# Router logits from turned x with folded norm weights; normed rows from two spread rows; two weight low halves on GpSimd

## The chip, the cores and the metric

The kernel runs on one core of a Trainium2 chip. The metric is the device time of one execution in microseconds, the median of the runs. The engines are TensorE (PE; its weight loads are PEld), VectorE (DVE), ScalarE (ACT), GpSimd (POOL) and SyncE (SP), which only issues DMAs; ScalarE and GpSimd issue DMAs as well.

## The reference, cut to what matters

Two token groups (256 latent tokens, 128 context tokens; 3 tiles of 128 rows) go through two layers of width 1024. A layer is a mixer (four token mixers, gated merge, output projection) and a mixture of experts, each behind a modulated norm:

```python
mod = silu(cond) @ w_mod + b_mod
sh1, sc1, g1, sh2, sc2, g2 = split(mod, 6)      # per group: c for latent, c_ctx for context
h = rmsnorm(x, norm_mix) * (1 + sc1) + sh1
x = x + g1 * mixer(h)
h = rmsnorm(x, norm_ffn) * (1 + sc2) + sh2
glog = h @ router_group                          # 4 groups, the best one is taken
elog = h @ router_expert                         # 16 experts, the best two of that group
...
gate = softmax weight of the group * normed softmax weights of the two experts
hid = silu(h @ w_gate) * (h @ w_up)
x = x + g2 * sum over experts (hid * gate) @ w_down
```

The change is in how the second `h` and the 20 logits `glog`, `elog` are made.

## The kernel before, in words

**Staging.** Weights come from HBM as units of 128x1024 fp32 (512 KB) through a ring of buffers. Large products are done in split form (`three`): an operand is written as a rounded high half and a low half (operand minus high half), and each product is `hi*hi + hi*lo + lo*hi` in three fp32r matmuls. ScalarE makes a unit's high half, GpSimd (mixer stage, line 812) or VectorE (expert stage, `unit_low`, line 1889) its low half; three units are in work at a time (`CONV`). In the mixer stage a unit takes TensorE about 4 us, in the expert stage about 1.4. The units of the output projection are the last eight of the mixer stage (`("gemm", 94)` to `("gemm", 101)`). After a unit stand the steps that `schedule()` puts there; each engine walks through the same `SCHEDULE` in order and skips what is not its own, so an engine that waits in a step does nothing of the later ones.

**Norm before the experts** (`("norm", 1)`, lines 1000 to 1042, 1444 to 1463, 1935 to 1982). When the projection of a tile is added to x (VectorE, line 1997 and below, `residual(t)`), ScalarE sums its squares, GpSimd makes 1/rms (`rstd`), VectorE and ScalarE scale the rows of x to `xn`. TensorE turns each of 8 chunks of 128 columns (`columns`), VectorE applies scale and shift per column, which now lie on partitions (line 1959), ScalarE and VectorE or GpSimd make high and low halves, TensorE turns the chunk back to rows (`back`), ScalarE copies it to `hn` (line 1021), and TensorE adds the chunk's part of the 20 logits in split form (`router`). Ahead of it TensorE has two groups of modulation products (`quad`, for the first chunks of the next layer; also run in the last layer), and runs of matmuls on the identity (`keep_busy`) fill gaps.

**Routing** (`("route",)`, lines 546 to 646, 1231 to 1238, 1493 to 1523). The logits (20 rows x 384 tokens) are copied by ScalarE, turned by TensorE to token rows and copied by VectorE (line 550). VectorE picks the group; TensorE counts tokens per group by a triangular matmul (line 1520); VectorE makes the selection matrices `sel` (line 579). TensorE then sorts the first 128 rows of group 0 by 24 matmuls `hn` x `sel` (line 1780). Meanwhile VectorE ranks the experts (lines 583 to 593), makes the gates and then the slot of every token in DRAM (to line 622); GpSimd writes `hn` and the gates to these slots with three indirect DMAs (line 888) and loads the next tile's rows `hs` (line 904).

**Experts.** Six tiles of 128 sorted rows, 24 units each: for expert e four gate/up units and two down units. `rows_high` (ScalarE) and `rows_low` (VectorE, line 1893) make the halves of the sorted rows. Order on VectorE at the start: `rows_low(0)`, gates, `rows_low(1)`, slots, low halves of units 3, 4, 5, then the loop with low halves and the hidden products of an expert (lines 2240 and 2244). Unit 8 of a tile is the first down unit (`S<-whi,ehi` in TensorE's rows). TensorE turns the next tile's rows behind unit 18 (line 1744).

**Queues.** SP issues in program order (lines 723 to 750): expert units 0 to 2, the next layer's modulation weights (`next_layer`), units 3 to 5 when the turned `xn` is read, units 6 to 11, then the gate of the experts spread on all partitions (`load_gate`). ScalarE issues the gate scratch stores (`gout`) and the spread of the first gate.

Of the kernel before, what the change touches and what calls it, by code (L numbers as in the profile page):

```python
# [22 lines left out]
F32 = mybir.dt.float32  # L23
# [5 lines left out]
P = 128  # L29
# [38 lines left out]
GRP = 4  # L68
# [29 lines left out]
BUSY_NORM, BUSY_LOGITS, BUSY_RANK, BUSY_PLACE = 5, 3, 5, 6  # L98
# [11 lines left out]
def schedule():  # L110
# [76 lines left out]
    put(36 + 30, ("gt", 0))  # L187
    put(36 + 33, ("gout", 0))
    put(36 + 50, ("gt", 1))
    put(36 + 53, ("gout", 1))  # L190
# [93 lines left out]
def program(nc, a, out, counts):  # L284
# [4 lines left out]
    with ctx:  # L289
# [13 lines left out]
        wlo = sb("wlo", [P, CONV, 1024], F32R)  # L303
        hhi = sb("hhi", [P, KD, TILES * P], F32R)
# [23 lines left out]
        h_sorted = nc.dram_tensor("h_sorted", (NT * P, ROW), F32, kind="Internal").ap()  # L328
        y_sorted = nc.dram_tensor("y_sorted", (NT * P, D), F32, kind="Internal").ap()
# [8 lines left out]
        smhi = sb("smhi", [P, KD, SMALL], F32R)  # L338
        smlo = sb("smlo", [P, KD, SMALL], F32R)
# [36 lines left out]
        rwf = rw[:, :, :].rearrange("p t n -> p (t n)")  # L376
        cond_t = prob[:, 0].rearrange("p a n -> p (a n)")[:, 0:32 * KD].rearrange("p (k c) -> p k c", k=KD)
# [68 lines left out]
        xn_act, hl_pool = sg("xn_act"), sg("hl_pool")  # L446
# [24 lines left out]
        nb_pe, nb_act = sg("nb_pe"), sg("nb_act")  # L471
# [10 lines left out]
        last_sel, last_selT, last_act, last_pe = sg("last_sel"), sg("last_selT"), sg("last_act"), sg("last_pe")  # L482
# [42 lines left out]

        def load_gate(queue, i):

            for c in range(2):
                src = a["g_scratch"][i].rearrange("(j c) n -> c j n", c=2)[c]
                g_in.of(queue.dma_start(gbc[:, c, :].rearrange("p (j n) -> p j n", j=KD),  # L530
                                        bass.AP(src.tensor, src.offset, [[0, P], [2 * P, KD], [1, P]])))
# [14 lines left out]
        def route(dve, need, own, tt, rows_low, next_mods, unit_low):  # L546

            V = nc.vector
            need(rt_pe, 0)
            own(V.tensor_copy(rt[:, :, :], O[:, 0:60].rearrange("p (t n) -> p t n", t=TILES)))  # L550
# [17 lines left out]
            rg_dve.of(tt(rw[:, :, 8:12], gl, b4(gmax), ALU.subtract))  # L568

# [11 lines left out]
            sel_dve.of(ins)  # L581

# [21 lines left out]
            rows_low(1)  # L604

# [20 lines left out]
            for n in range(CONV + 1, LEAD):  # L626
                unit_low(n)
# [22 lines left out]
        def _(sp):  # L650
# [11 lines left out]
            for l in range(layers):  # L662
# [33 lines left out]
                for s in SCHEDULE:  # L696
# [11 lines left out]
                    elif s == ("experts",):  # L708
# [15 lines left out]
                        for j in range(3):  # L724
                            next_layer(j)
# [1725 lines left out]
```

## Time and profile before

| | us |
|---|---|
| median of 3 runs | 1705.46 |
| lowest, highest | 1700.32, 1705.67 |
| the profiled execution | 1706.39 |
| its span, first to last instruction | 1704.8 |

Busy in the span: TensorE 1658.0 us (97%), VectorE 1014.5 (60%), ScalarE 871.0 (51%), GpSimd 657.1 (39%). The granted clock of TensorE was 0.993 of full on average.

A timeline row reads: start in us from the span's start, duration, engine, line of the kernel, operation, output tile <- input tiles, shape, count; in brackets the engine's idle time before it and what ended it. Rows of several instructions are merged; an fp32 matmul of TensorE that isn't a transpose leaves two records. A matmul's duration overlaps the next one's, so the pace is read from the starts. VectorE's rows of helper functions all carry the helper's line (1858), so they are told apart by their tiles. `pA` holds x and the expert units 0 to 2, `pB` the scaled rows and units 3 to 5.

### The profile page before, as it was taken

To read this page: it belongs to the slowest core of one execution; us is meant where nothing else is said; L and a number is where in the kernel's file an instruction comes from. 1 tells how busy PE (TensorE), PEld (TensorE's weight loads), DVE (VectorE), ACT (ScalarE), POOL (GpSimd) and SP (SyncE) were. 2 spreads that over 40 slices of the span, in tenths; PEclk is the share of its full clock that TensorE was granted. 3 is DMA by queue.
4 is the path that set the end of the run, shared out by engine and by line. 5 is a ranking of instruction groups with operands and counts; after the bars stand their busy time and mean duration, and the time that the engine had idled before them with its cause. 6 is when DMAs were issued, how large, how long until landed. Compare 5 with 4: busy or idle time off the path is not lost.

```text
span 1704.8 us, 27109 instructions
## 1 busy us (share of the span) xinstructions
PE 1658.0 (97%) x10021; PEld 1333.3 (78%) x10021; DVE 1014.5 (60%) x1736; ACT 871.0 (51%) x1471; POOL 657.1 (39%) x414
## 2 busy tenths in 40 slices
PE   6999999999999999999989999999999999999997
PEld 5788887777888877777768888777778887777775
DVE  2226567564451189999860384775635314899997
ACT  2443345544533357778634334454544234587884
POOL 0545464334476621001125554534346675111002
PEclk8999999999999999999999999999999999999999
DMA  8833344343556459999865334344354653999994
GB/s 310 284 103 107 107 148 124 106 180 136 206 202 210 173 210 403 373 369 369 310 224 187 99 115 142 107 131 141 131 192 149 244 198 115 365 385 366 372 364 156
DMA packets 120811, 367.13 MB, mean 215 GB/s; under 512 B 11964, under 2 KB 34044, under 8 KB 120704
## 3 DMA queue, kind: packets, MB, share of 16 engines
q1 hardware_dynamic: 95024, 323.99, 52.5%
q0 software_dynamic: 6624, 24.18, 3.8%
q10 hardware_dynamic: 19056, 17.52, 3.3%
q8 instruction: 69, 1.13, 0.3%
q14 instruction: 38, 0.31, 0.1%
HBM read 341.71 MB, written 23.93 MB: 214 GB/s over the span
## 4 chain that ended last, share of the span: by engine, by line
PE 71%; DVE 14%; issue 5%; ACT 4%; DMA 3%; POOL 1%; SPq 1%; ACTq 0%; DVEq 0%; POOLq 0%
PE G L1335 18%; PE G L1337 17%; PE G L1336 17%; DVE wlo L1858 6%; ACT whi L973 3%; DVE pA L1858 2%; PE T L1649 2%; PE O L1392 2%; DMA x_scratch<-pA 2%; PE S L1635 1%; PE O L1680 1%; PE S L1335 1%; DVE prob L1858 1%; PE S L1337 1%; PE S L1336 1%
## 5 line engine op out<-in xcount | busy, mean ns | idle before, releaser
L812 POOL TENSOR_TENSOR wlo<-raw,whi 128x1024 fp32r<-128x1024 f32 x198 | 488.8, 2474 | 561.2 <-ACT whi L965 561.2
L1335 PE MATMUL G<-whi,hhi 128*128 128x512 f32 (+1 forms) x1440 | 579.1, 402 | 11.2 <-DVE wlo L1858 5.4
L1337 PE MATMUL G<-whi,hlo 128*128 128x512 f32 (+1 forms) x1440 | 558.7, 388 | 0.0
L1336 PE MATMUL G<-wlo,hhi 128*128 128x512 f32 (+1 forms) x1440 | 558.4, 388 | 0.0
L1335 PEld LDWEIGHTS G<-whi,hhi 128*128 128x128 f32 x1440 | 271.4, 188 | 89.0 <-DVE wlo L1858 20.8
L1337 PEld LDWEIGHTS G<-whi,hlo 128*128 128x128 f32 x1440 | 271.3, 188 | 57.6
L1336 PEld LDWEIGHTS G<-wlo,hhi 128*128 128x128 f32 x1440 | 271.9, 189 | 47.3
L965 ACT ACTIVATE whi<-raw 128x1024 fp32r<-128x1024 f32 x204 | 214.7, 1054 | 103.2 <-PE G L1337 73.3
L1858 DVE TENSOR_TENSOR wlo<-raw,whi 128x1024 fp32r<-128x1024 f32 x150 | 179.7, 1219 | 6.7 <-ACT whi L973 3.7
L973 ACT ACTIVATE whi<-raw 128x1024 fp32r<-128x1024 f32 x144 | 152.7, 1061 | 33.1 <-PE G L1337 18.5
L973 ACT ACTIVATE whi<-pA 128x1024 fp32r<-128x1024 f32 x72 | 76.4, 1061 | 41.5 <-PE G L1337 22.9
L1858 DVE TENSOR_TENSOR wlo<-pA,whi 128x1024 fp32r<-128x1024 f32 x72 | 87.9, 1223 | 15.7 <-ACT whi L973 13.2
L1175 ACT ACTIVATE prob<-prob,am 128x384 f32<-128x384 f32 x64 | 38.9, 609 | 99.5 <-DVE am L1858 52.8
L1858 DVE TENSOR_TENSOR wlo<-pB,whi 128x1024 fp32r<-128x1024 f32 x72 | 85.3, 1223 | 6.9 <-ACT whi L973 6.3
L1335 PE MATMUL S<-whi,ehi 128*128 128x512 f32 x192 | 79.4, 413 | 6.8 <-DVE elo L1858 6.4
L973 ACT ACTIVATE whi<-pB 128x1024 fp32r<-128x1024 f32 x72 | 75.1, 1057 | 11.1 <-PE G L1337 10.7
L1335 PE MATMUL G<-whi,bhi 128*128 128x512 f32 x192 | 78.3, 408 | 0.0
L1337 PE MATMUL S<-whi,elo 128*128 128x512 f32 x192 | 75.3, 392 | 0.0
L1337 PE MATMUL G<-whi,blo 128*128 128x512 f32 x192 | 75.1, 391 | 0.0
L1336 PE MATMUL S<-wlo,ehi 128*128 128x512 f32 x192 | 75.1, 391 | 0.0
L1336 PE MATMUL G<-wlo,bhi 128*128 128x512 f32 x192 | 74.9, 390 | 0.0
L807 POOL TENSOR_TENSOR sink_col<-ones 128x1 f32<-128x1 f32 x26 | 15.4, 592 | 149.4 <-ACT yo L1271 76.7
(385 smaller groups left out, 2349.9 us busy)
## 6 DMA issues: line engine op xcount, KB each, us to landing
raw<-in_units SPq DMA_DIRECT2D x426, 512.0 KB, 5.0
pA<-in_units SPq DMA_DIRECT2D x78, 512.0 KB, 6.0
pB<-in_units SPq DMA_DIRECT2D x72, 512.0 KB, 6.3
h_sorted<-sig POOLq DMA_DIRECT2D x12, 514.0 KB, 7.2
hs<-h_sorted POOLq DMA_DIRECT2D x10, 514.0 KB, 7.5
y_sorted<-yo POOLq DMA_DIRECT2D x10, 512.0 KB, 7.2
bias<-in_nat_bias ACTq DMA_DIRECT2D x16, 256.0 KB, 3.6
kT<-in_units SPq DMA_DIRECT2D x6, 512.0 KB, 4.7
```

What stands on the lines that cost most here:

```text
L812: lo_done.of(nc.gpsimd.tensor_tensor(wlo[:, k, :], raw[:, POS_OF[g] % RAW, :], whi[:, k, :].bitcast(F32), ALU.subtract))
L965: hi_done.of(nc.scalar.activation(whi[:, g % CONV, :], raw[:, p % RAW, :], ACT.Copy))
L973: hi_done.of(nc.scalar.activation(whi[:, n % CONV, :], expert_raw(n), ACT.Copy))
L1175: e = nc.scalar.activation(prob[:, u % 2, m, lo:lo + w], src, ACT.Exp, bias=am[:, u % 2, i:i + 1], accum_out=am[:, u % 2, 4 + i:5 + i])
L1335: nc.tensor.matmul(dst, st_hi, mv_hi, start=start, stop=False)
L1336: nc.tensor.matmul(dst, st_hi, mv_lo, start=False, stop=False)
L1337: return nc.tensor.matmul(dst, st_lo, mv_hi, start=False, stop=stop)
L1392: mm = nc.tensor.matmul(O[32 * q:32 * q + 32, c0:c0 + P], cond[:, k, :], raw[:, MODPOS[j - MQ + 1 + q] % RAW, k * P:(k + 1) * P], start=(k ...
L1635: nc.tensor.matmul(S[:, m, 0:256], q, kT[r, kj, 0:256], start=True, stop=True)
L1649: mm = nc.tensor.transpose(T[:, m, b * P:(b + 1) * P], prob[:, u % 2, m, b * P:(b + 1) * P], ident[:, :])
L1680: mm = nc.tensor.matmul(O[64 * m:64 * m + 64, to], values(b, lo, 64), pr, **fl)
L1858: return V.tensor_tensor(o, i0, i1, op)
```

## The change

- **Router.** The logits are computed from x itself. Since `h = x * rstd * a + b` (`a = 32 * (1 + sc2) * norm_ffn` per column, `b = sh2`), the logit is `rstd * (x @ (a*W)) + b @ W`. `rsm` = `a*W` is made once per layer for each token group (two VectorE products behind `("modt", 4)`), `b @ W` by 8 small matmuls (`("rbias", 0)`) and spread over the partitions by two more (`("rbias", 1)`). TensorE turns x: the first 512 columns in the new step `("xt",)` between units 100 and 101, the others in `("norm", 1)` as each tile's residual is done. ScalarE copies turned x to `xT`. 24 plain fp32 matmuls with turned x as the stationary side (128x128) and 20 moving columns give the logits with tokens on partitions. The split router, the copy and the turning of the logits go.
- **Rows.** `hn = (x * a_row) * rstd + b_row` on VectorE: `part_row` for half a tile (a product of 128x512), `whole_row` for a tile (one scalar_tensor_tensor of 128x1024). a and b are turned (`("gt", 1)`, `("gt", 2)`), stored to scratch and spread over the partitions by four DMAs on ScalarE's queue (`rowsA`, `rowsB`) into `pB`. Whole row 0 comes behind the part rows, whole row 1 behind the group choice, whole row 2 behind `sel`. Scaling by columns, turning back and the copies to `hn` go in `("norm", 1)`.
- **Low halves.** GpSimd makes those of expert units 1 and 2 (VectorE did before), after whole row 2. VectorE makes unit 0's ahead of the evacuation of the last projection units, unit 3's ahead of the slot arithmetic and unit 4's in the middle of it.
- **TensorE.** The modulation quads run behind the logits and behind the group counts, and in the first layer only. Three of the four runs of `keep_busy` in this stretch go. The gate selection moves behind unit 3 of the first expert tile, which is written out instead of being the loop's first pass.
- **SP.** Units 6 to 11 are asked for before the gate (in the first layer 8 to 10 last, when the quads are read), the gate's spread before units 3 to 5, and these wait for whole row 2. In the last layer the next layer's modulation weights aren't loaded.

```diff
+    for i, at in enumerate((66, 71, 79, 86)):
+        put(at, ("gt", i))
+        put(at + 3, ("gout", i))
+    put(84, ("dma", "rowsA"))
+    put(88, ("rbias", 0))
+    put(90, ("rbias", 1))
+    put(FIRST_UNIT[CHUNK_NO["wout", 0]] + 2, ("dma", "rowsB"))
+    put(FIRST_UNIT[CHUNK_NO["wout", 1]] + 2, ("xt",))
...
# route(), VectorE
-            own(V.tensor_copy(rt[:, :, :], O[:, 0:60].rearrange("p (t n) -> p t n", t=TILES)))
+            own(*(V.scalar_tensor_tensor(rt[:, t, :], logit_bank(t), st[:, t:t + 1], rt[:, t, :],
+                                         ALU.mult, ALU.add) for t in range(TILES)))
...
             rg_dve.of(tt(rw[:, :, 8:12], gl, b4(gmax), ALU.subtract))
+            whole_row(1)
...
             sel_dve.of(ins)
+            whole_row(2)
...
             rows_low(1)
+            low_of_two()
+            unit_low(CONV)
...
             own(V.scalar_tensor_tensor(diff, base, float((GRP - 1) * P), at, ALU.add, ALU.subtract))
+            unit_low(CONV + 1)
...
             need(sg_pe, 0)
-            unit_low(CONV)
             q_gate.of(V.tensor_copy(gate[:, :], O[:, 0:GRP]))
-            for n in range(CONV + 1, LEAD):
+            for n in range(CONV + 2, LEAD):
                 unit_low(n)
...
# SP
+                        for r in (0, 1, 5) if more_layers else range(RAW):
+                            released(last_of(r))
+                            expert_load(RAW + r, RAW)
+                        need(*evacuated(CHUNK_NO["wout", 1], TILES - 1))
+                        sp.wait_ge(*g_out.at(l, 3))
+                        load_gate(sp, 3)
+                        need(router_dve, WHOLE + TILES - 1)
                         for n in range(TILES, RAW):
                             expert_load(n, 0)
+                        if more_layers:
+                            need(nx_pe, NEXT - 1)
+                            for r in (2, 3, 4):
+                                expert_load(RAW + r, RAW)
...
# GpSimd, ("norm", 1)
+                            pool.wait_ge(*router_dve.at(l, WHOLE + TILES - 1))
+                            pool.wait_ge(*e_lo.in_tile(l, 0, UT, 0))
+                            for n in (1, 2):
+                                pool.wait_ge(*hi_done.at(l, NG + n))
+                                e_lo.of(nc.gpsimd.tensor_tensor(wlo[:, n % CONV, :], expert_raw(n),
+                                                                whi[:, n % CONV, :].bitcast(F32), ALU.subtract))
...
# ScalarE, ("xt",) and ("norm", 1)
+                def turned_x(t, hf):
+                    act.wait_ge(*router_pe.at(l, TURNED_X + TILES * hf + t))
+                    router_act.of(nc.scalar.activation(xT[:, 4 * hf:4 * hf + 4, t * P:(t + 1) * P],
+                                                   psum(turn_bank(t, hf)).rearrange("p (c n) -> p c n", c=4), ACT.Copy))
...
# TensorE
+                def turn_x(t, hf):
+                    need(*((ev_pool, pooled(CHUNK_NO["wout", 0], t)) if hf == 0 else residual(t)))
+                    b = turn_bank(t, hf)
+                    free(b)
+                    for c in range(4):
+                        mm = nc.tensor.transpose(psum(b)[:, c * P:(c + 1) * P],
+                                                 x[:, t, (4 * hf + c) * P:(4 * hf + c + 1) * P], ident[:, :])
+                    router_pe.of(mm)
+                    read[b] = (router_act, COPIED_X + TILES * hf + t)
...
+                def logits(t, hf):
+                    need(router_dve, ROUTER_W)
+                    need(router_act, COPIED_X + TILES * hf + t)
+                    for k in range(4 * hf, 4 * hf + 4):
+                        mm = nc.tensor.matmul(logit_bank(t), xT[:, k, t * P:(t + 1) * P], rsm[:, k, t // 2, :],
+                                              start=(k == 0), stop=(k == KD - 1))
+                    return mm
...
# TensorE, ("norm", 1)
+                            for t in range(2):
+                                turn_x(t, 1)
+                            free("O")
+                            for hf in range(2):
+                                for t in range(2):
+                                    logits(t, hf)
+                            turn_x(2, 1)
+                            for hf in range(2):
+                                mm = logits(2, hf)
+                            rt_pe.of(mm)
...
# VectorE
+                def part_row(t, hf):
+                    h = slice(hf * 512, (hf + 1) * 512)
+                    own(tt(hn[:, t, h], x[:, t, h], rows[0][:, t // 2, h], ALU.mult))
...
+                def whole_row(t):
+                    dve.wait_ge(*rstd_pool.at(l, TILES + t))
+                    router_dve.of(V.scalar_tensor_tensor(hn[:, t, 0:D], hn[:, t, 0:D], st[:, t:t + 1], rows[1][:, t // 2, :],
+                                                       ALU.mult, ALU.add))
...
                         if i == n - 1 and kind == "wout":
+                            if arg == 1:
+                                unit_low(0, 0)
                             dve.wait_ge(*g_in.at(l, 1))
```

## Rows read from the trace of the kernel before

**Rows 1.** the page's part 4, shares of the chain that ended last, by engine

```profile
PE 71%; DVE 14%; issue 5%; ACT 4%; DMA 3%; POOL 1%; SPq 1%; ACTq 0%; DVEq 0%; POOLq 0%
```

**Rows 2.** timeline of TensorE, second layer, from the last projection unit on

```profile
1435.43 0.39 PE L1337 MATMUL G<-whi,hlo 128*128 128x512 f32 x1
...
1458.05 2.92 PE L1780 MATMUL T<-prob,hn 128*128 128x128 f32 x24 [0.43 <-DVE prob L579]
...
1464.38 0.49 PE L1335 MATMUL G<-whi,hhi 128*128 128x512 f32 x1
...
1478.09 0.49 PE L1335 MATMUL S<-whi,ehi 128*128 128x512 f32 x1 [1.68 <-DVE elo L1858]
...
1494.29 0.60 PE L1744 MATMUL T<-ident,hs 128*128 128x128 f32 x4
```

**Rows 3.** timeline of TensorE, first layer, the same two edges

```profile
599.22 0.39 PE L1337 MATMUL G<-whi,hlo 128*128 128x512 f32 x1
...
628.17 0.48 PE L1335 MATMUL G<-whi,hhi 128*128 128x512 f32 x1
```

**Rows 4.** timeline of VectorE, second layer, evacuation to expert units 4 and 5

```profile
1433.19 0.69 DVE L1858 TENSOR_TENSOR sig<-G,pC 128x512 f32<-128x512 f32 x1 [12.97 <-PE G L1337]
...
1436.58 0.69 DVE L1858 TENSOR_TENSOR pA<-pA,sig 128x512 f32<-128x512 f32 x1
...
1454.07 0.22 DVE L550 COPY rt<-O 128x60 f32<-128x60 f32 x1
...
1455.35 0.17 DVE L1858 TENSOR_TENSOR rw<-rt,rw 128x12 f32<-128x12 f32 x1
1456.22 0.17 DVE L574 COPY rw<-O 128x12 f32<-128x12 f32 x1 [0.71 <-PE O L1520]
...
1457.82 0.17 DVE L1858 TENSOR_TENSOR rw<-rt,rw 128x16 f32<-128x16 f32 x1
...
1461.63 0.69 DVE L1858 TENSOR_TENSOR hlo<-T,hhi 128x512 fp32r<-128x512 f32 x1
...
1467.57 0.17 DVE L622 TENSOR_SCALAR slot_at<-rw 128x3 int32<-128x3 f32 x1
...
1468.87 2.35 DVE L1858 TENSOR_TENSOR wlo<-pB,whi 128x1024 fp32r<-128x1024 f32 x2
```

**Rows 5.** timeline of TensorE, second layer, transposes between two projection units

```profile
1395.73 0.82 PE L1706 MATMUL T<-ident,pA 128*128 128x128 f32 x6
...
1396.97 0.48 PE L1335 MATMUL G<-whi,bhi 128*128 128x512 f32 x1
```

**Rows 6.** timeline of ScalarE, second layer, high halves of weight units

```profile
1423.67 1.06 ACT L965 ACTIVATE whi<-raw 128x1024 fp32r<-128x1024 f32 x1 [3.02 <-PE G L1337]
...
1466.06 1.06 ACT L973 ACTIVATE whi<-pB 128x1024 fp32r<-128x1024 f32 x1 [1.78 <-PE G L1337]
```

**Rows 7.** the page's part 6, DMA issues: KB each, us to landing

```profile
pB<-in_units SPq DMA_DIRECT2D x72, 512.0 KB, 6.3
...
hs<-h_sorted POOLq DMA_DIRECT2D x10, 514.0 KB, 7.5
```

**Rows 8.** timeline of GpSimd: a low half in the mixer, the row load

```profile
1037.68 2.40 POOL L812 TENSOR_TENSOR wlo<-raw,whi 128x1024 fp32r<-128x1024 f32 x1 [1.28 <-ACT whi L965]
...
1483.46 0.61 POOL L904 DMA_DIRECT2D hs<-h_sorted  x1
```

**Rows 9.** timeline of VectorE beside the low half of the group above

```profile
1038.05 0.15 DVE L1858 TENSOR_TENSOR ms<-S,ms 128x4 f32<-128x4 f32 x1
...
1038.84 1.25 DVE L1858 TENSOR_TENSOR ms<-ms 128x4 f32<-128x4 f32 x1
```

**Rows 10.** busy time by stretch; last columns: PEclk, DMA share, GB/s

```profile
862.00:864.00 2.00, 0.00 (x0) 0.01 (x1) 1.11 (x4) 1.88 (x2) 0.71 (x2) 1.00 0.92 352
864.00:866.00 2.00, 1.95 (x12) 1.57 (x12) 1.42 (x5) 0.45 (x1) 0.00 (x0) 0.73 0.98 365
866.00:870.00 4.00, 2.06 (x5) 1.68 (x6) 4.00 (x9) 1.19 (x4) 0.00 (x0) 0.50 0.95 352
```

More of the change, by code:

```diff
@@ L1454, in _ @@
-                        for c in range(KD if w else 4):
-                            columns(w, c)
-                            if w and c:
-                                back(c - 1)
-                            if w and c > 1:
-                                router(c - 2)
-                        if w:
-                            back(KD - 1)
-                            router(KD - 2)
-                            router(KD - 1)
+                        if w:
+                            for t in range(2):
[8 more added lines that the diff above has]
+                            rt_pe.of(mm)
+                            continue
@@ new lines, in _ @@
+                        keep_busy(S[:, 0, 0:P], BUSY_BEGIN)
+                        need(xn_dve, 1)
+                        need(xn_act, 0)
+                        for c in range(4):
+                            columns(c)
+                    elif s == ("xt",):
+                        for t in range(TILES):
+                            turn_x(t, 0)
+                    elif s == ("rbias", 0):
+                        need(mod_dve, 3)
+                        free("O")
+                        for k in range(KD):
+                            mm = nc.tensor.matmul(O[0:2, 0:NLOG], modc[:, 3, k, :], small[:, k, 16:SMALL],
+                                                  start=(k == 0), stop=(k == KD - 1))
+                        router_pe.of(mm)
+                        read["O"] = (router_act, BIAS_COPY)
+                    elif s == ("rbias", 1):
+                        free("O")
+                        for c in range(2):
+                            mm = nc.tensor.matmul(O[:, c * NLOG:(c + 1) * NLOG], ident[0:2, c:c + 1].to_broadcast([2, P]), qrow,
+                                                  start=True, stop=True)
+                        router_pe.of(mm)
+                        read["O"] = (router_dve, ROUTER_BIAS)
@@ L1746, in turn, with one_tile @@
                                 q_t.of(mm)
-                        def one_tile(i, last):
+                        def one_tile(i, last, first=False):
                             pe.wait_ge(*q_lo.in_tile(l, i, 2, 0))
@@ L1762, in one_tile @@
                                     down(i, e, u - 4)
+                                if n == SELECT_GATES and first:
+                                    need(gates_dve, 0)
+                                    for t in range(TILES):
+                                        mm = nc.tensor.matmul(O[:, 0:GRP], sel[:, t, :], hn[:, t, D:ROW],
+                                                              start=(t == 0), stop=(t == TILES - 1))
+                                    sg_pe.of(mm)
                                 if n in TURN_HID:
@@ L1783, in _ @@
                             q_t.of(mm)
-                        need(gates_dve, 0)
-                        for t in range(TILES):
-                            mm = nc.tensor.matmul(O[:, 0:GRP], sel[:, t, :], hn[:, t, D:ROW],
-                                                  start=(t == 0), stop=(t == TILES - 1))
-                        sg_pe.of(mm)
-                        with pe.Fori(0, NT - 1) as i:
+                        if l < DEPTH - 1:
+                            turned()
+                        one_tile(0, False, True)
+                        with pe.Fori(1, NT - 1) as i:
                             one_tile(i, False)
```

296 lines of the change are left out of this document (143 added, 153 removed).

## Prediction

> **What bounds the kernel now.** I read the chain that ended last first [rows 1]: TensorE carries 71% of it, VectorE 14%, so a stretch is worth what it keeps TensorE from starting. The diff touches one such stretch per layer, between the output projection and the expert matmuls. TensorE's timeline of the second layer [rows 2]: the last projection matmul starts at 1435.43; such matmuls stand 0.23 us apart, so I set E = 1435.66 and count from it. Sorting starts at E+22.4, the first expert matmul at E+28.7, the first down matmul (unit 8) at E+42.4, after 1.68 us of waiting for VectorE. In the first layer the distance is the same, 628.17 - 599.45 = 28.7 [rows 3]. All that the change can touch is some 42 us in each of two layers. I follow it to unit 8, because VectorE paces the first expert tile. VectorE's rows [rows 4] show the order there: evacuation of the projection, 1433.19 to 1437.27; logits taken over at 1454.07; group choice out at 1455.52; counts back at 1456.22; ranking from 1457.82; first low half of the sorted rows at 1461.63; slots at 1467.57.
>
> **Part 1, work moved ahead of E.** TensorE gets 12 transposes (first half of x) between two projection units. The same insertion, 12 transposes between units, took from 1395.73 to 1396.97 [rows 5], and 0.08 for the slower restart: 1.3 us. The logits' shift needs 8 fp32 matmuls with a stationary side of two columns, 16 records; no row shows such. Bounds: nothing, if they slip into the gaps, and 0.117 a record, the pace of the 54 records (24 sorting matmuls, 3 of the gate selection, two records each) between 1458.05 and 1464.38 [rows 2], 1.9 in all. I take 1.0: the nearest row has 128 columns to load and these have two, but each record must still be issued. Two spreading matmuls (4 records, 0.5) and two more transposes of 16 rows (0.1 each by [rows 5]): **3.0 us** per layer, bounds 2.0 to 3.9. This is on the path: TensorE runs those units back to back. Two more scratch stores, four spread loads and the copies lie on ScalarE, which waits about 3 us in every unit [rows 6]: nothing; without that cover some 3 us. VectorE's three products of the first half go where it idles for 12.97 us [rows 4]. They keep the shared port for 3 x 0.69 = 2.1 us from GpSimd, whose low halves are about as much ahead: nothing, at most 0.5 without the cover. SP now loads expert units 3 to 5 when the third whole row is done (E+14.2), behind two spread loads; such a load lands 6.3 us later [rows 7] and ScalarE wants it after unit 0, at about E+25: nothing, with 4 us of cover.
>
> **Part 2, E to sorting.** ScalarE now has three copies of turned x before the high half of expert unit 0, and VectorE makes unit 0's low half ahead of the evacuation, so that starts at about E-0.95 instead of 1433.19 = E-2.5. At (1437.27-1433.19)/3 = 1.36 us a tile the residuals are done at E+0.4, +1.8 and +3.1. TensorE turns tiles 0 and 1 (to E+2.3), then has 16 logit matmuls. A sorting matmul is the nearest, 2 records of 0.117: 0.23 us each, 3.7, to E+6.0; four transposes 0.45; 8 matmuls 1.85: E+8.3, seen by VectorE at E+8.45. Meanwhile VectorE has three half products (0.72 each with their waits) and whole row 0, E+3.1 to E+6.6: hidden. A whole row costs what a low half of the same 1024 elements does, 2.35/2 = 1.2 us [rows 4]. From the logits to the group choice it was 1.45 us, now 1.65 (three instructions for one copy): E+10.1. Whole row 1 takes 1.2 and covers the wait of 0.70 for the counts: E+11.3. From there to sorting it was 1458.05 - 1456.22 = 1.83; whole row 2 adds 1.2: sorting starts at **E+14.35, 8.05 us earlier**. The old norm on turned rows (16 scalings, 8 highs, 8 lows, 24 transposes back, 24 split matmuls) is gone from the path; the second layer's two modulation quads, gone too, lay beside other work.
>
> **Part 3, sorting to the first expert matmul.** Before: 1458.05 to 1464.38, 6.3 us. The gate selection (6 records, 0.7) moves behind unit 3, so TensorE could start 5.6 after 14.35, at E+20.0. But GpSimd's two low halves are released by whole row 2, just when the ranking starts, and one takes 2.4 us [rows 8]. In [rows 9], beside such an operation, VectorE's product with one operand in PSUM takes 0.15 us; the later one, as small but with both operands in SBUF, starts at 1038.84 and ends at 1040.09, when GpSimd is done at 1040.08: 1.25 us. The ranking is a chain with such products all along. One runs before GpSimd starts, the next waits out the first low (2.2 us), the third the second low (2.2). The Trainium skill, "SBUF — State Buffer", section "SBUF: two separate sides", calls this port pair an exclusive lock, held for the full instruction. By that rule the sum is the one that follows; with a split of bandwidth it would be rival 1's. The ranking, 1457.82 to 1461.63 = 3.8 us, becomes 8.2; the first low of rows (0.69) ends at E+14.2+8.2+0.7 = E+23.1, and the first expert matmul is at **E+23.3**, 5.4 us earlier than 28.7.
>
> **Part 4, first expert tile** (S is its first matmul). VectorE now makes unit 3's low half before the slot arithmetic. It can't start before the high half, which ended 2.7 us after the first expert matmul (1466.06+1.06 [rows 6]); the slot arithmetic (2.8 us, to 1467.74) had filled that wait. Now gates and the second low of rows come first and fit; VectorE idles to S+2.8; low 3 to S+4.0, arithmetic 1.4, low 4, arithmetic 1.4, low 5 to S+9.15. Before, low 5 ended at 1471.2 = S+6.8. The order after it is unchanged, so unit 8, 13.7 after S before, comes at S+15.9: **2.2 us** lost. Bounds: 0, if TensorE has slack that I don't see, and 2.8.
>
> **Sum per layer**, at unit 8: before E+42.4; after 3.0 + 23.3 + 15.9 = 42.2. That is -0.2 us, -0.5 for both with rounding. The profiled execution took 1706.39 (span 1704.8), the median of the runs is 1705.46; set against the median: **1705.0 us**. About 0.3%, 5.1 us, is what a measurement of this kernel can tell from no change.
>
> **Rivals.** 1. *The low halves don't hold up the ranking.* Then S = E+20.0 and each layer wins 3.5: 1705.5 - 7.1 = 1698.4. For it: products with PSUM pass freely, and reductions may. Against: [rows 9]. If part 4 costs nothing too and part 1 its lower bound, each layer wins 3.5+2.2+1.0 = 6.7: 1692.
> 2. *TensorE's clock falls in the stretch* (the slow side). From E to E+2.3 it has 0.9 us of transposes, three runs of filler matmuls are gone, in the second layer the quads too; and it idles 3.3 us before the first expert matmul. [rows 10]: after 862 to 864 without work the granted clock was 0.73, then 0.50 of full, the lower level, 1.2 GHz. If one fall per layer keeps 6.8 us of path work there (half of the first 2 us, the next 4, and a rest), it loses 3.4 us of full-speed work: 1705.0+6.8 = 1711.8. It decides from 5.6 us lost in all, so it needs a fall in both layers, ahead of sorting. Just before the first expert matmul it costs some 1.1 a layer, since VectorE is the later one there; that stays within the forecast. Against: the gap of 1.68 us at unit 8 [rows 2] was followed by matmuls at full pace.
> 3. *The next tile's rows come late.* GpSimd issued that load at 1483.46 [rows 8], it lands in 7.5 [rows 7], 1491.0; TensorE read at 1494.29 [rows 2], 3.3 to spare. Slots come at S+7.9 instead of S+3.4, TensorE's reading at +2.2: 1.0 is left. This adds 0 to 1.5 us per layer to the forecast: up to 1708.
>
> **Chances.** Forecast, with rival 3: 0.45, its own range 1701 to 1709. Rival 1: 0.22, with its better terms 0.09. Rival 2: 0.16. The other 0.08 are misjudged sizes, either way. Faster by over 0.3%: 0.32; within: 0.47; slower: 0.21. The range leaves out half of the best case and what goes past one fall per layer: 1696.5 to 1712.
>
> **What would show it.** Right: sorting at about E+14 and the first expert matmul at about E+23 in both layers; two GpSimd lows right behind the third whole row; the second and third ranking product some 2.3 us long; TensorE idle some 3 us before the first expert matmul; low 5 some 9 us behind it. Wrong: ranking products of 0.17 us beside GpSimd's (rival 1); a granted clock below 1.00 between E and sorting (rival 2); TensorE waiting for tile 1's rows (rival 3). Sorting later than E+16 at full clock would mean that a logit matmul costs more than 0.23 us, or that the evacuation is held longer.

## The result and the profile after

The changed kernel takes 1708.1 us (median of 20 runs, 1705.2 to 1713.4) against 1704.95 us for the kernel before (median of 20 runs beside them). The ratio is 1.0027, 95% interval 1.0020 to 1.0033: 4.6 us slower (3.4 to 5.6). The forecast was 1705.0, no change. With 20 executions of each kernel the interval is much finer than the 0.3% that the prediction took as the least that can be told from no change. The profiled execution took 1707.19 us. The mean granted clock, from the view of cores, before and after:

```profile
core 0: 1704.8 us, clock 0.993
```

```profile
core 0: 1705.6 us, clock 0.987
```

The spans differ by only 0.8 us, and that is luck of these two executions, as two rows of TensorE's timeline show in each, the first gate matmul of the first and of the second layer (T). Before, then after:

```profile
61.79 0.34 PE L1335 MATMUL O<-hhi,smhi 128*16 128x384 f32 x1
...
897.59 0.34 PE L1335 MATMUL O<-hhi,smhi 128*16 128x384 f32 x1
```

```profile
59.19 0.34 PE L1392 MATMUL O<-hhi,smhi 128*16 128x384 f32 x1
...
896.34 0.34 PE L1392 MATMUL O<-hhi,smhi 128*16 128x384 f32 x1
```

What the change doesn't touch, the program's start and the passage between the layers (from its last fillers to the next T, 39.9 before and 38.1 after), took 2.6 us (61.79 - 59.19) and 1.8 us less in the later execution. The clock was at its lower level there for 6.8 us instead of 13.7, and for 3.4 instead of 6.8, summed over windows of half a us. It isn't the change that does it: e9_wide below, with the same program up to there, starts as slowly as the kernel before (T at 61.39). Between these points the two traces compare piece by piece (E as in the prediction, unit 8 is the first down matmul):

| stretch, us | before, layer 1 / 2 | after, layer 1 / 2 |
|---|---|---|
| T to E | 537.7 / 538.1 | 540.8 / 540.8 |
| E to sorting | 22.4 / 22.4 | 18.6 / 17.9 |
| E to first expert matmul | 28.7 / 28.7 | 26.5 / 26.1 |
| E to unit 8 | 42.4 / 42.4 | 42.3 / 41.8 |
| unit 8 to the layer's last fillers | 215.8 / 215.7 | 216.0 / 216.1 |

Ahead of E each layer loses 3.1 and 2.7; behind it the change gives back 0.1 and 0.7; the rest adds 0.2 and 0.4. That is +5.6 us, and the ratio says +4.6 (3.4 to 5.6). So the question is why unit 8 comes at E+42.3 and E+41.8, when the forecast had E+39.2. The answer stands in the windows of the first layer (stretch, length, TensorE busy and instructions, granted clock, share of the DMA engines, GB/s):

```profile
599.00:602.00 3.00, 2.07 (x12) 1.00 0.00 0
602.00:605.00 3.00, 3.00 (x29) 0.93 0.42 122
605.00:608.00 3.00, 3.00 (x16) 0.50 0.81 233
608.00:611.00 3.00, 3.00 (x19) 0.50 0.00 0
611.00:614.00 3.00, 3.00 (x61) 0.50 0.00 0
614.00:617.00 3.00, 3.00 (x80) 0.86 0.02 5
```

From 604.6 (E+4.6) to 614.8 (E+14.9) the granted clock is at the lower level, 1.2 GHz, while TensorE is busy all the time. The kernel before has the full clock in this place, in both layers, though TensorE waits there too:

```profile
599.00:620.00 21.00, 19.90 (x242) 1.00 0.25 83
...
1435.00:1456.00 21.00, 19.92 (x242) 1.00 0.26 89
```

The second layer after the change on TensorE's timeline, against [rows 2]:

```profile
1436.92 0.39 PE L1394 MATMUL G<-whi,hlo 128*128 128x512 f32 x1
1437.57 0.66 PE L1432 MATMUL S<-ident,pA 128*128 128x128 f32 x4 [0.26 <-DVE pA L1926]
1438.90 0.66 PE L1432 MATMUL T<-ident,pA 128*128 128x128 f32 x4 [0.67 <-DVE pA L1926]
1439.39 0.97 PE L1442 MATMUL O<-rsm,xT 128*128 128x20 f32 x8
1440.20 1.29 PE L1442 MATMUL G<-rsm,xT 128*128 128x20 f32 x8
...
1444.74 1.09 PE L1432 MATMUL T<-ident,pA 128*128 128x128 f32 x4
1445.63 3.44 PE L1442 MATMUL G<-rsm,xT 128*128 128x20 f32 x16
1451.03 0.60 PE L1565 MATMUL O<-rw,tri 128*128 128x12 f32 x2 [1.96 <-DVE rw L1926]
...
1455.02 4.31 PE L1850 MATMUL T<-prob,hn 128*128 128x128 f32 x24 [0.21 <-DVE hn L1968]
...
1463.24 0.50 PE L1392 MATMUL G<-whi,hhi 128*128 128x512 f32 x1 [1.23 <-DVE hlo L1926]
...
1478.90 0.50 PE L1392 MATMUL S<-whi,ehi 128*128 128x512 f32 x1 [1.44 <-DVE elo L1926]
```

E = 1437.15. The first logit group takes 0.81 us (1439.39 to 1440.20, four matmuls, 0.20 each), the last one 3.44 for eight, 0.43 each: half the pace. The logits end at E+11.9 instead of E+8.3, sorting starts at E+17.9 instead of E+14.35. The fall was there in both layers: in the second the clock was low from E+3.7 to E+20.8.

The other large term came as forecast. GpSimd's two lows and VectorE's ranking products:

```profile
1455.05 4.65 POOL L876 TENSOR_TENSOR wlo<-pA,whi 128x1024 fp32r<-128x1024 f32 x2 [11.10 <-DVE hn L1968]
```

```profile
1454.88 0.17 DVE L1926 TENSOR_TENSOR rw<-rt,rw 128x16 f32<-128x16 f32 x1
...
1455.30 2.12 DVE L1926 TENSOR_TENSOR rw<-rt,rw 128x16 f32<-128x16 f32 x1
1457.46 0.18 DVE L622 TENSOR_REDUCE rw<-rw 128x4 f32<-128x16 f32 x1
1457.67 2.06 DVE L1926 TENSOR_TENSOR rw<-rt,rw 128x16 f32<-128x16 f32 x1
...
1466.10 1.23 DVE L1926 TENSOR_TENSOR wlo<-pB,whi 128x1024 fp32r<-128x1024 f32 x1 [1.00 <-ACT whi L1014]
```

The first product takes 0.17 us, the second and third 2.12 and 2.06: they end when the first and when the second of GpSimd's operations ends (4.65 us for the two). The reduction between them passes in 0.18. It is the picture of [rows 9], where the product came in the middle of GpSimd's operation and so waited for 1.25 us only. VectorE idles only 1.00 us ahead of low 3.

### The profile page after: what moved, and what is told of

It is laid out like the page before. It is cut to its first block, busy times and chain, and to the rows that moved or that the text cites. A ratio compares the mean times of both kernels' runs of the same rounds, so it can differ in the third digit from the quotient of the medians.

```text
span 1705.6 us, 26714 instructions
## 1 busy us (share of the span) xinstructions
PE 1654.6 (97%) x9871; PEld 1334.5 (78%) x9871; DVE 1022.5 (60%) x1714; ACT 859.0 (50%) x1452; POOL 659.8 (39%) x412
## 4 chain that ended last, share of the span: by engine, by line
PE 73%; DVE 14%; issue 5%; ACT 4%; DMA 2%; SPq 1%; POOL 1%; ACTq 0%; DVEq 0%; POOLq 0%
PE G L1392 19%; PE G L1394 17%; PE G L1393 17%; DVE wlo L1926 5%; ACT whi L1014 3%; DVE pA L1926 2%; PE T L1713 2%; PE O L1468 2%; PE O L1744 2%; PE S L1699 2%; DMA x_scratch<-pA 1%; PE S L1392 1%; PE S L1394 1%; PE S L1393 1%; DVE prob L1926 1%
## 5 line engine op out<-in xcount | busy, mean ns | idle before, releaser
L1392 PE MATMUL G<-whi,hhi 128*128 128x512 f32 (+1 forms) x1440 | 579.0, 402 | 15.9 <-DVE wlo L1926 7.2
L1014 ACT ACTIVATE whi<-raw 128x1024 fp32r<-128x1024 f32 x144 | 152.6, 1060 | 38.1 <-PE G L1394 24.1
L1926 DVE TENSOR_TENSOR wlo<-pA,whi 128x1024 fp32r<-128x1024 f32 x68 | 83.3, 1225 | 32.3 <-ACT whi L1014 30.7
L933 POOL TENSOR_TENSOR gate<-hs,ones 128x4 f32<-128x4 f32 x10 | 7.0, 696 | 169.6 <-PE G L1808 169.6
```

What stands on the lines that cost most here:

```text
L1014: hi_done.of(nc.scalar.activation(whi[:, n % CONV, :], expert_raw(n), ACT.Copy))
L1392: nc.tensor.matmul(dst, st_hi, mv_hi, start=start, stop=False)
L1926: return V.tensor_tensor(o, i0, i1, op)
```

## The experiments

Each run is timed against the kernel before on one chip. The table gives the ratio, its 95% interval, the median over the executions of the mean granted clock, and E to unit 8 in the profiled execution:

| run | ratio | interval | clock | layer 1 / 2 |
|---|---|---|---|---|
| the change | 1.0027 | 1.0020 to 1.0033 | 0.987 | 42.3 / 41.8 |
| e1_fill | 1.0036 | 1.0023 to 1.0050 | 0.988 | 40.1 / 39.7 |
| e2_dlow | 1.0010 | 0.9998 to 1.0023 | 0.987 | 39.9 / 38.6 |
| e3_slot | 1.0062 | 1.0049 to 1.0076 | 0.984 | 43.7 / 43.1 |
| e4_all3 | 1.0023 | 1.0011 to 1.0036 | 0.989 | 40.1 / 43.2 |
| e5_fillmore | 1.0026 | 1.0014 to 1.0038 | 0.991 | 44.2 / 39.7 |
| e6_fillwaits | 1.0025 | 1.0014 to 1.0037 | 0.991 | 42.7 / 42.2 |
| e7_dlow_slot | 0.9995 | 0.9982 to 1.0009 | 0.987 | 39.1 / 38.2 |
| e8_best | 1.0015 | 1.0005 to 1.0026 | 0.991 | 41.3 / 36.9 |
| e9_wide | 0.9978 | 0.9969 to 0.9986 | 0.994 | 38.3 / 38.1 |
| e10_widewaits | 0.9988 | 0.9980 to 0.9997 | 0.995 | 38.6 / 38.5 |
| e11_best2 | 0.9955 | 0.9942 to 0.9968 | 0.994 | 35.4 / 35.1 |
| e12_nofill | 0.9941 | 0.9928 to 0.9955 | 0.993 | 34.9 / 36.3 |

**First: fillers among the logits.**

```diff
+free("S0")
 for t in range(2):
+    keep_busy(S[:, 0, 0:P], 2)
     turn_x(t, 1)
+keep_busy(S[:, 0, 0:P], 2)
 free("O")
 for hf in range(2):
     for t in range(2):
         logits(t, hf)
+        keep_busy(S[:, 0, 0:P], 1)
 turn_x(2, 1)
+keep_busy(S[:, 0, 0:P], 2)
```

> Edit: twelve filler matmuls of 128 columns more in each layer, between the last projection matmul E and the logits of the third tile (two before each of the first two groups of transposes, two before the logits, one behind each of the four logit groups of tiles 0 and 1, two before the logits of tile 2). Theory (the granted clock is what the forecast missed): no fall between E and sorting in either layer, mean granted clock 0.993 instead of 0.987; the fillers lie on the path with some 1.4 us, the others in waits; sorting at E+15.8 (after the change: E+17.9, in the first layer E+18.6), first expert matmul at E+24.7 (E+26.1, E+26.5), unit 8 at E+40.5 (E+41.8, E+42.3): about 1.5 us less a layer, 1705 us. Rival (a logit matmul of 20 columns costs more than 0.23 us at any clock): the fillers only add 1.4 us a layer, sorting past E+19, 1711 us.

In the profiled execution it went as the clock theory said up to sorting: the logits at full pace, sorting at E+15.85 in both layers, unit 8 at E+40.1 and E+39.7. The theory's "no fall" didn't hold even there: in the second layer the clock was low from E+11.7 to E+18.5, behind 1.96 us without work, which unit 8 doesn't show. And that was the fastest of seven executions; the others went up to 1713.3 with clocks down to 0.984, and the median is no better than the changed kernel's. So one profile would have misled. That the others lost their time in the logits fits the runs below, but their clocks are means over the whole execution and don't show the place.

**GpSimd's lows.** VectorE makes them while it waits for the logits.

```diff
-    for n in (1, 2):
-        pool.wait_ge(*hi_done.at(l, NG + n))
-        e_lo.of(nc.gpsimd.tensor_tensor(wlo[:, n % CONV, :], expert_raw(n),
-                                        whi[:, n % CONV, :].bitcast(F32), ALU.subtract))
...
 whole_row(0)
+unit_low(0, 1)
+unit_low(0, 2)
```

> Edit: VectorE instead of GpSimd makes the low halves of expert units 1 and 2, right behind whole row 0, while it waits for the logits. Theory (GpSimd's operation keeps VectorE out): second and third ranking product 0.1 to 0.2 us instead of 2.1, the ranking 3.9 us shorter, both lows done at E+9, before the logits come at E+12; the first expert matmul is then set by the end of sorting, E+24.9: 1.2 us earlier in the second layer and about 2 in the first, 1705 us. Rival (the products are slow for another reason, or the lows on VectorE delay the route): no gain or a loss of 1 us a layer, 1708 to 1710.

The lock theory holds. VectorE's rows of the second layer:

```profile
1454.34 0.17 DVE L1919 TENSOR_TENSOR rw<-rt,rw 128x16 f32<-128x16 f32 x1
...
1454.76 0.18 DVE L1919 TENSOR_TENSOR rw<-rt,rw 128x16 f32<-128x16 f32 x1
```

These are the second and the third product, which had taken 2.12 and 2.06 us. The first expert matmul comes at E+23.0 in the second layer, behind sorting without a wait (in the change it waited 1.23 us for VectorE), and E to unit 8 is 2.5 and 3.1 us shorter. Of the 3.1, 1.0 is no gain of this edit: the clock fell 1.0 us later in that layer, and sorting started at E+16.9 instead of E+17.9. From sorting to the first expert matmul the two layers gain 2.5 and 2.1. The ratio, 1.0010 against 1.0027, is 2.9 us better; the two intervals overlap by a hair.

**The slot arithmetic ahead again.**

```diff
-unit_low(CONV)
 own(V.tensor_scalar(tiles, size, 128.5, None, ALU.is_gt))
...
-unit_low(CONV + 1)
...
 slot_dve.of(V.tensor_scalar(slot_at[:, :].unsqueeze(2), slot, -1.0, None, ALU.add))
+unit_low(CONV)
 need(sg_pe, 0)
 q_gate.of(V.tensor_copy(gate[:, :], O[:, 0:GRP]))
-for n in range(CONV + 2, LEAD):
+for n in range(CONV + 1, LEAD):
     unit_low(n)
```

> Edit: the slot arithmetic stands ahead of the low half of expert unit 3 again, as in the kernel before; all else as changed. Theory: VectorE idles only 1.0 us before that low half in this trace, so the 2.8 us of arithmetic hide 1.0 at most: unit 8 comes 0.8 to 1.0 us earlier a layer, 1706.4 us. Rival A (the 2.2 us a layer of the forecast are all there): 1703.7. Rival B (unit 8 is set by something else): 1708.1.

Missed by all of them: slower, and the rows name a wait that I had overlooked. VectorE, then TensorE:

```profile
636.78 0.16 DVE L661 COPY gate<-O 128x4 f32<-128x4 f32 x1 [2.31 <-PE O L1829]
```

```profile
638.22 0.47 PE L1391 MATMUL G<-whi,hhi 128*128 128x512 f32 x1 [1.48 <-DVE wlo L1925]
```

The change also moved the gate selection behind unit 3 on TensorE. VectorE takes the gates over ahead of low 4, so with the old order of VectorE it idles 2.31 us with two lows queued behind the copy, and TensorE waits 1.48 us for them. The change's two moves belong together. E to unit 8 grew by 1.35 and 1.4 us. Against the change the ratio is 0.0035 higher, 6 us; in the profiled execution 3.5 of its 6.7 us stand at the program's start (2.2) and between the layers (1.3), which the edit doesn't touch. Why all five executions are that slow, with clocks down to 0.982, is open.

**The three together** were built with the same flaw.

> Edit: the edits of the three runs before together. Theory: sorting at E+15.8, ranking 3.8 us, first expert matmul at E+22, unit 8 at 13.7 behind it, E+35.8 instead of E+42: 6.3 us less a layer, 1695.5 us. Rival (the gains don't add up, since one wait takes the place of another): the sum of each alone, 1700 us, or above.

In the first layer the first expert matmul was at E+21.9, as forecast, but unit 8 18.2 us behind it, by the wait of e3_slot. In the second the clock fell at E+7 in spite of the fillers.

**More fillers, and fillers in waits alone.** Beside those of e1_fill: 7 in the second layer ahead of the counts, `BUSY_PLACE` 8 and 14 for 6, and 8 behind sorting. e6_fillwaits leaves out the ones behind the groups of logits and the two ahead of the first group.

> Edit: on the changed kernel, ten filler matmuls of 128 columns between E and the logits of tile 2 (one of them behind each logit group of tiles 0 and 1), and more where TensorE only waits: 7 in the second layer ahead of the counts, 8 and 14 instead of 6 behind them, 8 behind sorting. Theory (the clock; the earlier run with twelve fillers had E to unit 8 in 40.0 us, but its other executions had granted clocks down to 0.984): mean granted clock 0.992 or more in all executions, E to unit 8 in 39.8 us, median 1703.5 us. Rival (the falls do not depend on what stands in this stretch): clocks from 0.984 to 0.990 again, median 1708.

> Edit: the fillers of the run before, but none between the groups of logits, only where TensorE waits for another engine. Theory A (waits lose the clock): no fall, the logits end 1 us earlier, E to unit 8 in 39 us, median 1702. Theory B (matmuls of 20 columns lose it, though TensorE is busy all along with them): the fall stands in the logits as in the changed kernel, they end at E+11 to E+12, E to unit 8 in 41.8 us, 1707 to 1708.

Windows of e5_fillmore, the logits of the first and of the second layer:

```profile
606.00:609.00 3.00, 3.00 (x20) 0.65 0.56 166
609.00:612.00 3.00, 3.00 (x17) 0.50 0.00 0
...
1442.00:1445.00 3.00, 3.00 (x29) 1.00 0.95 284
1445.00:1448.00 3.00, 3.00 (x30) 1.00 0.24 64
```

One layer fell and one did not. Where it falls, the fillers themselves run at half pace, and E to unit 8 is 44.2, longer than in the change; where not, 39.7. In this profile the mean of the two is the change's 42, and over the executions too the time stayed, though the clock rose to 0.991. In e6_fillwaits both layers fell. TensorE had no idle time in the windows of the fall nor in the one ahead of it; before that it had waited for 0.2 us since E (597.90 in the first layer):

```profile
600.00:603.00 3.00, 3.00 (x30) 1.00 0.49 143
603.00:606.00 3.00, 3.00 (x18) 0.53 0.73 211
606.00:609.00 3.00, 3.00 (x16) 0.50 0.00 1
...
1442.00:1445.00 3.00, 3.00 (x17) 0.50 0.04 11
```

That is Theory B: waits are not what loses the clock here. The Trainium skill, "TensorE: Matmul & The Clock Gate", section "HAM oscillation — how this bites in real kernels", puts falls in the middle of a kernel down to waits for data between groups of matmuls; by that rule this run should not have fallen, and the trace disagrees: busy 3.00 us in 3.00 at a granted clock of 0.50. Counted over the profiles: with 20 columns and no fillers between the groups the clock fell within the logits in 10 of 10 layers (the change, e2, e3, e6, e7); with fillers between them in 3 of 8 (e1, e4, e5, e8). These are four profiles against five, so 3 of 8 says that such fillers don't prevent the fall, and not how often they do.

**VectorE's order, with the gates last**, on top of the edit of e2_dlow.

```diff
-unit_low(CONV)
...
-unit_low(CONV + 1)
...
-need(sg_pe, 0)
-q_gate.of(V.tensor_copy(gate[:, :], O[:, 0:GRP]))
-for n in range(CONV + 2, LEAD):
+for n in range(CONV, LEAD):
     unit_low(n)
+need(sg_pe, 0)
+q_gate.of(V.tensor_copy(gate[:, :], O[:, 0:GRP]))
```

> Edit: VectorE makes the lows of units 1 and 2 behind whole row 0 (no GpSimd), and the slot arithmetic stands ahead of the lows of units 3, 4 and 5, with the gates taken over behind them, so that none of the lows waits for the gate selection, which the change moved behind unit 3. Theory: VectorE idles 1.24 us ahead of low 3 in the run with the lows alone (1462.99), and that is what the arithmetic hides: unit 8 at 14.5 us behind the first expert matmul instead of 15.7, 1.2 us less a layer than that run, 1702.3. Rival A (the 2.2 us of the forecast): 13.5, 1700.3. Rival B (as in the earlier run with the arithmetic ahead: TensorE gets unit 3 later and loses): 17, 1707.

Unit 8 comes 15.0 and 15.2 us behind the first expert matmul, against 15.75 and 15.6 in e2_dlow: 0.8 and 0.45 us, neither the 1.2 of the theory nor the 2.2 of my forecast. Against e2_dlow the ratio is 0.0015 lower, with intervals that overlap. VectorE's low halves of units 3 to 5 in the second layer, where the first expert matmul is at 1460.07:

```profile
1464.32 3.49 DVE L1917 TENSOR_TENSOR wlo<-pB,whi 128x1024 fp32r<-128x1024 f32 x3
```

Low 5 ends 7.7 us behind the first expert matmul, against 9.15 in e2_dlow. It gains 1.4, and unit 8 only 0.45 of it.

> Edit: the two lows by VectorE and the order of the run before, with the fillers of the first of these four but the 8 behind sorting. Theory: sorting at E+16.3, first expert matmul at E+21.9, unit 8 at E+36.4 in both layers, 6 us less than in the kernel before, of which the work ahead of E takes 3.0: 1703.5 - 6 = 1697.5. Rival (the clock falls all the same): 1702.

As e5: the first layer fell (E to unit 8 in 41.3), the second did not (36.9, forecast 36.4). It measured 1705.2: the rival's fall, at 3 us more than the rival's 1702.

**The columns of a logit matmul.** One edit, nothing added or moved:

```diff
-mm = nc.tensor.matmul(logit_bank(t), xT[:, k, t * P:(t + 1) * P], rsm[:, k, t // 2, :],
+mm = nc.tensor.matmul(six_banks(t), xT[:, k, t * P:(t + 1) * P],
+                      rsm[:, k, t // 2, :].unsqueeze(1).to_broadcast([P, 6, NLOG]),
...
```

> Edit: on the changed kernel, each of the 24 logit matmuls a layer streams its 20 columns six times over (120 columns, the last 100 of the result are not used); nothing is added or moved. By the rows of the changed kernel a record of 20 columns and one of 128 take the same 0.12 us at full clock, so at one clock the time is unchanged. Theory B (the matmuls of 20 columns lose the clock though TensorE is busy with them): no fall between E and sorting, logits end at E+8.4, sorting at E+14.4, first expert matmul at E+23.3, unit 8 at E+39.1: 2.9 us less a layer than the 42 of the changed kernel, mean granted clock 0.992 or more; the kernel before is at 1703.5 on this chip and the changed one some 4.6 above it, so 1702.3. Rival (the waits, or chance): falls as before, clock 0.987, 1708.

> Edit: the 120 columns of the run before, and filler matmuls where TensorE waits for another engine (two before each of the first two groups of transposes, two before the logits of tile 2, 7 in the second layer ahead of the counts, 8 and 14 instead of 6 behind them, 8 behind sorting). If the columns and the waits both count: clock 0.994 or more, E to unit 8 in 39.1 us in both layers in nearly every execution, 1701.5. If the columns alone decide: the same as the run before within 1 us. If neither: 1708.

The second layer of e9_wide, the logits and sorting, and then the windows of both layers:

```profile
1436.58 1.05 PE L1446 MATMUL O<-rsm,xT 128*128 128x120 f32 x8
1437.46 1.06 PE L1446 MATMUL G<-rsm,xT 128*128 128x120 f32 x8
...
1448.52 4.62 PE L1855 MATMUL T<-prob,hn 128*128 128x128 f32 x24 [0.81 <-DVE hn L1973]
```

```profile
606.00:609.00 3.00, 3.00 (x29) 1.00 0.99 299
609.00:612.00 3.00, 3.00 (x76) 1.00 0.17 40
...
1439.00:1442.00 3.00, 3.00 (x29) 1.00 0.87 253
1442.00:1445.00 3.00, 1.04 (x10) 1.00 0.00 0
1445.00:1448.00 3.00, 2.72 (x14) 0.54 0.00 0
```

A matmul of 120 columns takes 0.22 us (0.88 for four), one of 20 took 0.20; six times the columns cost 0.02. With that, sorting is at E+14.2 in both layers and unit 8 at E+38.3 and E+38.1 (expected 39.1). The waits and the transposes ahead of the logits are those of the change, so neither can be what loses the clock there. The ratio falls from 1.0027 to 0.9978, intervals apart: 8.3 us, where the two profiles' sum of E to unit 8 shows 7.7. e6_fillwaits and e10_widewaits differ in the columns alone too: 1.0025 and 0.9988, intervals apart. In the four runs with 120 columns, 0 of 8 layers fell within the logits. What e9_wide still shows is a fall in each layer, behind a wait: in the second at E+11, behind a window with 1.04 us of work in 3, in the first at E+24, behind the 2.39 us in which TensorE waits for VectorE ahead of the first expert matmul. Those are a matter of waits: the fillers of e10_widewaits took them away (clock 0.995, no low window between E and unit 8), but unit 8 came 0.3 and 0.4 us later and the ratio was no better. The second layer of e12_nofill below has such a fall at E+10.4 too, and unit 8 at 36.3 against the first one's 34.9.

**The columns and GpSimd's lows together.** 120 columns, VectorE's lows, ScalarE's high half of unit 2 ahead of its work for tile 2, and the order of e7_dlow_slot; with the fillers of e10_widewaits but for the last 8, and without any.

```diff
 turned_x(t, 1)
+if w and t == 1:
+    need(*unit_done(NG - 1))
+    high(0, 2)
...
-    need(*unit_done(NG - 1))
-    high(0, 2)
```

> Edit: 120 columns and the fillers in waits (without the 8 behind sorting), the lows of units 1 and 2 on VectorE behind whole row 0, ScalarE's high half of unit 2 ahead of its work for tile 2, slot arithmetic and gates as in the run e7_dlow_slot. Theory: sorting at E+14.8, first expert matmul at E+20.4, unit 8 at E+35.5; 6.9 us less than before in each layer, of which 3.0 go to the work ahead of E: 1703.5 - 7.8 = 1695.7. Rival (the clock falls in about every second layer, as with fillers among the logits): 1700.

> Edit: the run e11_best2 without any of its added fillers (120 columns a logit matmul, lows of units 1 and 2 on VectorE, high half of unit 2 earlier, the slot order). The runs with 120 columns, without and with fillers, stood at 1700.2 and 1701.7. If the columns alone keep the clock up: within 1.5 us of e11_best2's ratio to the kernel before (0.9955), clock 0.992 or more. If the fillers carry a part of it here, where GpSimd's lows are gone and sorting is followed at once by the expert matmuls: a fall in some stretches, ratio 0.997 or above. Against the run with 120 columns alone (ratio 0.9978) the difference is the price of GpSimd's lows and the order of VectorE at full clock: 2.5 to 4 us.

1695.9 us with the fillers and 1694.1 without (5 executions each), where the kernel before stood at 1703.6 and 1703.7: ratios 0.9955 and 0.9941. Both beat both kernels; the second takes 0.6% less than the kernel before. It is 2.4 us below e11_best2 where at most 1.5 was expected, with intervals that overlap: here too the fillers won nothing. Rows of e12_nofill, first layer (E = 601.76):

```profile
621.72 0.48 PE L1388 MATMUL G<-whi,hhi 128*128 128x512 f32 x1
...
636.70 0.50 PE L1388 MATMUL S<-whi,ehi 128*128 128x512 f32 x1 [1.62 <-DVE elo L1923]
```

Sorting starts at E+14.4, the first expert matmul follows it without a wait at E+20.0, unit 8 comes at E+34.9. Against e9_wide the ratio is 0.0037 lower, 6.3 us, more than the 2.5 to 4 expected. The two profiles show 5.2 of it, 3.8 ahead of the first expert matmul and 1.4 behind it. How the 3.8 divide between GpSimd's lows and the earlier high half of unit 2 was not separated; e2_dlow, without the latter, gained 2.5 and 2.1 there.

## Why the prediction was wrong

The measured 1708.1 lies inside the stated range, and that is no support: the forecast was no change, and 4.6 us clear of noise were lost by a fall of the clock that part 2 had left out. That the miss stays small is partly luck, since the forecast is too high in other terms. With the clock kept in the logits (e9_wide) the change takes 3.8 us less than the kernel before (2.4 to 5.3), and not the 0.5 of the forecast.

**Part 1 was right.** T to E grew by 3.1 and 2.7 us against a forecast of 3.0. Of its terms the rows confirm the transposes and correct the shift:

```profile
1378.12 0.56 PE L1520 MATMUL O<-small,modc 128*2 128x20 f32 x16
1378.61 0.50 PE L1392 MATMUL G<-whi,hhi 128*128 128x512 f32 x1
...
1387.00 0.62 PE L1527 MATMUL O<-rw,ident 2*128 2x20 f32 x4
...
1431.71 1.04 PE L1432 MATMUL T<-ident,pA 128*128 128x128 f32 x8
1432.58 0.60 PE L1432 MATMUL S<-ident,pA 128*128 128x128 f32 x4
1432.93 0.48 PE L1392 MATMUL G<-whi,hhi 128*128 128x512 f32 x1
```

The transposes cost 1.22 (forecast 1.3), the 16 records of the shift 0.49 (forecast 1.0), the spread 0.54 (forecast 0.5; the next matmul starts at 1387.54). With the forecast's 0.2 for the two transposes of 16 rows that is 2.45 us; the other 0.6 in the first layer and 0.3 in the second lie elsewhere ahead of E, and no row was read for them.

**Part 2 is the step that failed**, and in it one term: the logits at 0.23 us each up to E+8.3. Everything ahead of it held: the evacuation began at E-1.04 (forecast E-0.95), the residuals ended at E+0.4, +1.7 and +3.0. At full clock the term holds too, as e9_wide shows with logits until E+8.2 and sorting at E+14.2 (forecast E+14.35). But matmuls of 20 columns did not keep the full clock, and the last ones took 0.43 us: E+11.9, sorting at E+17.9 and E+18.6.

**Rival 2** was that fall, and its chance of 0.16 was too small; its size (3.4 us a layer, both layers, 1711.8) was near: sorting came 3.5 and 4.2 us late, of which 2.6 and 3.1 were left at unit 8 (41.8 and 42.3 against 39.2). I had argued against it with the gap at unit 8, where matmuls went on at full pace behind a wait. That is evidence on waits, and this fall needs none. I counted the 0.9 us of transposes and the fillers that go, and not the 24 matmuls of 20 columns as something that could lose the clock itself; no row of before showed such a stream. Nor are the missing fillers shown as its cause: put back in the waits alone (e6_fillwaits) they did not prevent it, and without them 120 columns kept the clock in the logits (e9_wide, e12_nofill). They matter for the later falls, behind waits.

**Part 3 was right in its mechanism and some 0.9 us too dear**: two products of 2.1 us (forecast 2.2 each), and a whole ranking of 7.7 us (forecast 8.2). The Trainium skill, "SBUF — State Buffer", section "SBUF: two separate sides", calls the pair of ports an exclusive lock; the rows here and in e2_dlow agree, 2.12 against 0.17 for the same product. Rival 1 falls. TensorE's idle time ahead of the first expert matmul was forecast at about 3 us and measured 2.2 in the first layer and 1.2 in the second, where sorting still ran at the lower clock. At full clock the first layer of e9_wide has 2.39, and the first expert matmul stands at E+22.4 in both of its layers (forecast 23.3): that is most of the 1 us by which unit 8 comes earlier there than forecast.

**Part 4**: unit 8 came 15.8 and 15.7 us behind the first expert matmul (forecast 15.9), low 5 ended 9.2 behind it in the second layer (forecast 9.15). The size was right and the reason for the most part not. I put the 2.2 us (2.35 by the two ends of low 5 in the prediction) on the order of VectorE's work; e7_dlow_slot, with the arithmetic ahead of the lows and no wait on the gates, got back only 0.8 and 0.45. There low 5 came 1.4 earlier in the second layer and unit 8 only 0.45, so unit 8 doesn't follow low 5 one for one, as I had assumed. A part of the rest is that the first expert matmul stands closer to sorting, since the gate selection no longer stands between: VectorE starts the second low half of the rows 0.1 us ahead of it before and 0.9 behind it in e7_dlow_slot. What sets the remainder is open.

**Rival 3** did not happen: GpSimd issued the load of the next rows at 1486.06, and TensorE turned them at 1495.28 without a wait.

## What to carry to other kernels

When a stream of matmuls replaces another, look at how many columns each one streams, and not only at their number and the engine's busy time; broadcasting the 20 columns to 120 cost 0.02 us a matmul here and kept the clock in that stream. Judge a cure for the clock by the clock of all executions, since the one profile of e1_fill looked like a cure and the median showed none. Put GpSimd's operations on SBUF where VectorE waits anyway, not beside a chain of tiny VectorE products. When two steps of a change release each other, undoing one alone measures a new wait.

## What the runs showed of the hardware

- A stream of fp32 matmuls of 20 columns (128 rows, 128 columns of weights) was followed by the lower clock level in 10 of 10 layers although TensorE was busy 3.00 us in 3.00; the same stream with 120 columns in 0 of 8. The price a matmul: 0.20 us against 0.22 at full clock, and 0.43 for 20 columns at the low one.
- Fillers of 128 columns between groups of four such matmuls lowered that to 3 of 8, differently from layer to layer within one execution. What decides it there was not tried.
- Small VectorE products (128x16, both operands in SBUF) waited until GpSimd's operation on SBUF ended, 2.1 us instead of 0.17, twice in a row; reductions of one operand between them did not (0.18 us).
- The falls at the program's start and between the layers differ from one profile to the next, whatever is changed behind them: T of the first layer lies between 57.5 and 61.8, and the passage from the last fillers of the first layer to T of the second between 36.9 and 40.0 us.
